# Compressed keys and values of a hybrid decoder step: two tokens stacked on 128 rows, and the first attention scores laid between the stages

## The reference, cut to what matters

```
def nsa_compress(rows, w1, w2, pe):              # rows: tokens x 64, once for keys, once for values
    n_cmp = (L - CMP_LEN) // CMP_STRIDE + 1      # CMP_LEN = 32, CMP_STRIDE = 16
    idx = arange(n_cmp)[:, None] * CMP_STRIDE + arange(CMP_LEN)[None, :]
    blocks = rows[:, idx] + pe                   # windows of 32 tokens
    h = gelu(einsum('bnld,ldh->bnh', blocks, w1))    # w1: 32 x 64 x 128
    return einsum('bnh,hd->bnd', h, w2)              # w2: 128 x 64
```

## Time and profile before

| | us |
|---|---|
| median of 3 runs (lowest, highest) | 1422.31 (1421.23, 1422.4) |
| the profiled execution: its time | 1421.6 |
| its span, first to last instruction | 1419.7 |
| PE busy | 1290.8 (91%) |
| DVE busy | 712.4 (50%) |
| ACT busy | 405.0 (29%) |
| POOL busy | 177.3 (12%) |

### The profile page before, as it was taken

One profiled execution on the slowest core, in us unless ns is written; L12 is line 12 of the kernel. 1 busy time (PEld: TensorE's weight loads), 2 busy tenths in 40 slices (PEclk: granted clock), 3 DMA queues, 4 the chain that ended last, 5 costly groups with the idle time before them and its releaser, 6 DMA issues.

```text
span 1419.7 us, 19519 instructions
## 1 busy us (share of the span) xinstructions
PE 1290.8 (91%) x6942; PEld 774.6 (55%) x6942; DVE 712.4 (50%) x1629; ACT 405.0 (29%) x858; POOL 177.3 (12%) x209
## 2 busy tenths in 40 slices
PE   3699999999999999979999999999828999999966
PEld 1568787787877545646666765545323333333322
DVE  5526575574854101247676674253752333333339
ACT  3132232332421200115665664132201111111016
POOL 0003121030221000200000000000001222211132
PEclk9699999999999999969999999999958999999988
DMA  9802011040111205204300004500167968495855
GB/s 315 256 18 60 16 40 37 18 75 0 34 59 46 97 0 90 94 8 95 111 18 9 1 1 134 168 34 27 65 232 260 317 241 292 156 333 161 280 178 222
DMA packets 123238, 163.19 MB, mean 115 GB/s; under 512 B 29763, under 2 KB 98547, under 8 KB 123160
## 3 DMA queue, kind: packets, MB, share of 16 engines
q1 hardware_dynamic: 108840, 112.75, 26.1%
q0 software_dynamic: 14320, 49.41, 10.1%
HBM read 225.01 MB, written 36.45 MB: 184 GB/s over the span
## 4 chain that ended last, share of the span: by engine, by line
PE 79%; DVE 13%; DMA 3%; ACT 2%; issue 2%; POOL 0%; SPq 0%; DVEq 0%; POOLq 0%; ACTq 0%
PE act L652 16%; PE vec L1159 11%; PE vec L919 9%; PE vec L681 7%; PE vec L853 5%; PE vec L702 4%; PE act L865 4%; PE act L877 2%; PE act L1172 2%; PE vec L1172 2%; PE act L884 2%; DMA arena<-x_rows,arena 2%; PE vec L817 1%; PE vec L662 1%; PE act L1139 1%
## 5 line engine op out<-in xcount | busy, mean ns | idle before, releaser
L652 PE MATMUL act<-arena 128*128 128x352 f32 x768 | 240.2, 469 | 0.4 <-issue 0.4
L652 PEld LDWEIGHTS act<-arena 128*128 128x128 f32 x768 | 146.0, 194 | 77.6 <-issue 4.6
L1159 PE MATMUL vec<-arena 128*64 128x512 f32 x768 | 172.4, 601 | 2.5 <-issue 2.5
L919 PE MATMUL vec<-arena 128*128 128x512 f32 (+1 forms) x288 | 126.3, 593 | 0.4 <-ACT arena L1357 0.4
L1795 DVE CUSTOM_DVE_ANT_0 arena<-vec,arena 128x128 f32<-128x128 f32 (+9 forms) x200 | 86.8, 459 | 59.8 <-PE vec L853 49.7
L1159 PEld LDWEIGHTS vec<-arena 128*64 128x64 f32 x768 | 54.2, 138 | 103.9 <-issue 103.5
L681 PE MATMUL vec<-arena 128*128 128x512 f32 (+1 forms) x256 | 99.9, 546 | 0.0
L2087 DVE TENSOR_SCALAR arena<-arena 128x256 f32<-128x256 f32 x24 | 7.1, 296 | 170.7 <-ACT arena L1468 170.7
L919 PEld LDWEIGHTS vec<-arena 128*128 128x128 f32 (+1 forms) x288 | 50.8, 180 | 67.6 <-issue 66.3
L1370 ACT COPY arena<-act 128x512 f32<-128x512 f32 (+11 forms) x176 | 63.6, 431 | 81.3 <-PE act L865 81.3
L1377 ACT ACTIVATE arena<-arena 128x640 f32<-128x640 f32 (+15 forms) x128 | 81.6, 644 | 16.5 <-DVE arena L1795 16.5
(11 more groups left out here) (378 smaller groups left out, 1873.0 us busy)
## 6 DMA issues: line engine op xcount, KB each, us to landing
arena<-in_exp_w SPq DMA_DIRECT2D x144, 1024.0 KB
y_rows<-arena POOLq DMA_DIRECT2D x48, 256.0 KB, 5.1
arena<-in_w_in SPq DMA_DIRECT2D x16, 512.0 KB, 7.0
arena<-in_x_prompt SPq DMA_DIRECT2D x8, 512.0 KB, 8.9
x_spill<-arena POOLq DMA_DIRECT2D x8, 512.0 KB, 5.7
arena<-x_spill SPq DMA_DIRECT2D x8, 512.0 KB, 5.5
arena<-in_cache_fox_kv SPq DMA_DIRECT2D x16, 256.0 KB, 3.4
x_rows<-arena POOLq DMA_DIRECT2D x8, 512.0 KB, 2.9
```

Source lines behind the costliest of these rows:

```text
L652: last = mm(bk[:, 0:n], W[k % 2][:, c, m * P:(m + 1) * P], xT[:, c, a:a + n], start=c == 0, stop=c == NC - 1)
L919: last = mm(bk[:r], src, Wo[:, c, half * 512:(half + 1) * 512], start=c == 0, stop=c == NC - 1)
L1159: last = mm(gu_bank[p][o], xgT[p][:, c, o], Wgu[:, slot, c, :], start=c == 0, stop=c == NC - 1)
```

## The change

Two neighbouring tokens are stacked: rows 0 to 63 hold even tokens, rows 64 to 127 odd ones, keys and values in two planes of a new buffer, `tokens2`. The first layer is then 16 matmuls of 128 rows for keys and 16 for values, in place of 64 of 64 rows. Keys' hidden values come first, then the decay rows of head 0, then the values' hidden values; the rest of the compression is laid between the first steps of attention. The cached rows are loaded before `w1c`, which is loaded in four parts; the position rows are turned after the first sparse tile, the cached ones within the loop of tiles. The GELU is done for keys and for values apart (183 columns each). `cumf` and `foxdiag` move behind `S` and `PT` in memory.

```diff
@@ the stream of SP @@
-        e.wait_ge(*E.at(("w_in used", 5)))
-        e.dma_start(w1c[0:64], I["nsa_cmp_w1"][0, 0].rearrange("l d x -> d l x")).then_inc(*E.moved("cmp_in"))
-        e.dma_start(w1c[64:128], I["nsa_cmp_w1"][0, 1].rearrange("l d x -> d l x")).then_inc(*E.moved("cmp_in"))
...
         for n in range(DB * NP):
             e.dma_start(KVT[:, n // NP, n % NP, :], nkp[page_of(n), :, 0:2].rearrange("a p k d -> p (a k d)")).then_inc(*E.moved("cmp_cache_in"))
-        e.wait_ge(*E.at("KC ready"))
+        e.wait_ge(*E.at(("w_in used", 5)))
+        for kv in range(2):
+            for odd in range(2):
+                src = I["nsa_cmp_w1"][0, kv].rearrange("(j two) d x -> two d j x", two=2)
+                e.dma_start(w1c[64 * odd:64 * odd + 64, kv], src[odd]).then_inc(*E.moved("cmp_in"))
+        e.wait_ge(*E.at("VC ready"))
@@ the stream of PE @@
         for t in range(NT):
             token_tile(t, W_nkvg, 400, 6)
+            if t == 0:
+                e.wait_ge(*E.at("cmp_in"))
+                e.wait_ge(*E.free("vec"))
+                bk = E.bank("vec")
+                e.transpose(bk[:, 0:32], pe_sb[0:32, :], ident[0:32, 0:32]).then_inc(*E.filled("vec"))
+                e.wait_ge(*E.at("cmp_cache_in"))
+            if t % 2 and t < 8:
+                turn_cached_keys(t - 1)
             if t >= 2:
                 turn_sparse_keys(t - 2)
-        e.wait_ge(*E.at("cmp_cache_in"))
-        for b in range(0, DB, 2):
...
         turn_sparse_keys(7)
...
-        for l in range(32):
-            for kv in range(2):
-                s = slice(64 * kv, 64 * kv + 64)
-                last = mm(hidden_banks[kv][:, 0:WINDOWS], w1c[s, l, :], skew(kcvc[s, :], l, [16, WINDOWS]), start=l == 0, stop=l == 31)
+        def hidden_values(kv):
+            e.wait_ge(*E.free("vec"))
+            bk = E.bank("vec")
+            for j in range(16):
+                last = mm(bk[:, 0:WINDOWS], w1c[:, kv, j, :], skew(tokens2[:, kv, :], j, [8, WINDOWS]), start=j == 0, stop=j == 15)
+            last.then_inc(*E.filled("vec"))
...
+        hidden_values(0)
+        e.wait_ge(*E.at("LF ready"))
+        decay_rows(0)
+        hidden_values(1)
         E.stage("attn")
-        e.wait_ge(*E.at("KC ready"))
...
-        decay_rows(0)
         for d in range(n + 3):
+            if d == 1:
+                compressed_keys()
+                e.wait_ge(*E.at("KC ready"))
+            if d == 4:
+                e.wait_ge(*E.at("VC ready"))
             if d < n:
                 scores(d)
+                if d == 1:
+                    compressed_values()
@@ the stream of ACT @@
-            e.copy(KVT[:, b:b + 2].rearrange("p b j n -> p (b j n)"), bk).then_inc(*E.drained("act", "KVT ready"))
+            for kv in range(2):
+                turned = bk[64 * kv:64 * kv + 64].rearrange("p (t two) -> p t two", two=2)
+                for odd in range(2):
+                    last = e.copy(tokens2[64 * odd:64 * odd + 64, kv, at:at + PAST], turned[:, :, odd])
@@ the stream of DVE @@
+        def pairs_of(bk, n, at):
+            for kv in range(2):
+                turned = bk[64 * kv:64 * kv + 64, 0:n].rearrange("p (t two) -> p t two", two=2)
+                for odd in range(2):
+                    last = cp(tokens2[64 * odd:64 * odd + 64, kv, at // 2:(at + n) // 2], turned[:, :, odd])
...
-            cp(kcvc[:, t * P:(t + 1) * P], bk[:, 0:P]).then_inc(*E.done())
+            pairs_of(bk, P, t * P).then_inc(*E.done())
...
+        gelu_inner(0)
         decay_rows(0)
+        gelu_outer(0)
+        gelu_inner(1)
         for it in range(n + 1):
+            if it == 1:
+                compressed_keys()
             if it < n:
                 scores(it)
+                if it == 1:
+                    gelu_outer(1)
+                    compressed_values()
```

More of the change, by code:

```diff
@@ L267, in program @@
     w2, w2d, pe_sb, pc = z.take(2 * P, 2), z.take(2 * P), z.take(P), z.take(2)
-    w1c = z.take(32 * P, 32)
+    w1c = z.take(32 * P, 2, 16)
     tail = 53200 - 2 * 4096 - NC * NTOK
@@ L777, in turn_sparse_keys, with turn_cached_keys @@
             bk = E.bank("vec")
-            for j, a in enumerate((0, 64, 192)):
-                last = e.transpose(bk[:, j * P:(j + 1) * P], nkvg[:, t, a:a + P], ident)
+            for n, a in enumerate((0, 64, 192)):
+                last = e.transpose(bk[:, n * P:(n + 1) * P], nkvg[:, t, a:a + P], ident)
             last.then_inc(*E.filled("vec"))
+        def turn_cached_keys(b):
+            e.wait_ge(*E.free("act"))
+            bk = E.bank("act")
+            for n in range(4):
+                last = e.transpose(bk[:, n * P:(n + 1) * P], KVT[:, b + n // NP, n % NP, :], ident)
+            last.then_inc(*E.filled("act"))
         e.wait_ge(*E.at(("w_in", 5)))
@@ L829, in _ @@
[L829 to L833, removed]
+        e.wait_ge(*E.at("pairs by vec"))
+        e.wait_ge(*E.at("pairs by act"))
+        def hidden_values(kv):
+            e.wait_ge(*E.free("vec"))
+            bk = E.bank("vec")
+            for j in range(16):
+                last = mm(bk[:, 0:WINDOWS], w1c[:, kv, j, :], skew(tokens2[:, kv, :], j, [8, WINDOWS]), start=j == 0, stop=j == 15)
+            last.then_inc(*E.filled("vec"))
@@ new lines, in compressed_keys, with compressed_values @@
+        def compressed_keys():
+            e.wait_ge(*E.at(("cmp hidden", 0)))
+            e.wait_ge(*E.free("vec"))
+            bk = E.bank("vec")
+            mm(bk[:, 0:HALF_GELU], w2d[:, 0:P], gx[:, 0:HALF_GELU], start=True, stop=True).then_inc(*E.filled("vec"))
+        def compressed_values():
+            e.wait_ge(*E.at(("cmp hidden", 1)))
+            e.wait_ge(*E.free("vec"))
+            bk = E.bank("vec")
+            v = gx[:, HALF_GELU:]
+            mm(bk[:NCMP, 0:64], v[:, 0:NCMP], w2[:, 1, 0:64], start=True, stop=True).then_inc(*E.filled("vec"))
+            e.wait_ge(*E.free("vec"))
+            bk = E.bank("vec")
+            for b in range(DB):
+                last = mm(bk[:NCMPS, b * 64:(b + 1) * 64], v[:, NCMP + 15 * b:NCMP + 15 * b + 15], w2[:, 1, 0:64], start=True, stop=True)
+            last.then_inc(*E.filled("vec"))
@@ L1334, in _ @@
             bk = E.job("act")
[L1335 removed]
+            at = (NTOK + b * PAST) // 2
+            for kv in range(2):
+                turned = bk[64 * kv:64 * kv + 64].rearrange("p (t two) -> p t two", two=2)
+                for odd in range(2):
+                    last = e.copy(tokens2[64 * odd:64 * odd + 64, kv, at:at + PAST], turned[:, :, odd])
+                    last.then_inc(*(E.drained("act", "pairs by act") if kv and odd else E.done()))
         e.wait_ge(*E.at("gate logits"))
@@ L1343, in _ @@
         E.stage("p3")
[L1344 to L1348, removed]
+        for kv in range(2):
+            u = gu[:, kv * HALF_GELU:(kv + 1) * HALF_GELU]
+            e.wait_ge(*E.at(("gelu inner", kv)))
+            act(u, u, ACT.Exp, scale=-1.5957691216057308).then_inc(*E.done(("gelu exp", kv)))
         E.stage("attn")
@@ L1675, in _ @@
         e.memset(tmp9, 0.0).then_inc(*E.done())
+        def pairs_of(bk, n, at):
+            for kv in range(2):
+                turned = bk[64 * kv:64 * kv + 64, 0:n].rearrange("p (t two) -> p t two", two=2)
+                for odd in range(2):
+                    last = cp(tokens2[64 * odd:64 * odd + 64, kv, at // 2:(at + n) // 2], turned[:, :, odd])
+                    if not (kv and odd):
+                        last.then_inc(*E.done())
+            return last
         def sparse_keys_turned(t):
@@ L1733, in gelu, with compressed_keys, compressed_values @@
             e.wait_ge(*E.own())
-            tt(x, x, u, ALU.mult).then_inc(*E.done(tag))
-        for kv in range(2):
+            tt(x, x, u, ALU.mult).then_inc(*E.done(("cmp hidden", kv)))
+        def compressed_keys():
             e.wait_ge(*E.full("vec"))
             bk = E.job("vec")
[L1739 to L1756, removed]
+            cp(KC[64:128, 0:NCMP], bk[64:128, 0:NCMP]).then_inc(*E.done())
+            cp(KCs[64:128, :], bk[64:128, NCMP:HALF_GELU]).then_inc(*E.drained("vec", "KC ready"))
+        def compressed_values():
+            e.wait_ge(*E.full("vec"))
+            bk = E.job("vec")
+            cp(VC[:NCMP, :], bk[:NCMP, 0:64]).then_inc(*E.drained("vec"))
+            e.wait_ge(*E.full("vec"))
+            bk = E.job("vec")
+            cp(VCs[:NCMPS], bk[:NCMPS].rearrange("p (b d) -> p b d", b=DB)).then_inc(*E.drained("vec", "VC ready"))
         E.stage("attn")
```

62 lines of the change are left out of this document (25 added, 37 removed).

## The result

The changed kernel took 1426.56 us (median of 9 runs, 1423.87 to 1432.01), the kernel before 1422.40 in the same series: ratio 1.0036, 95% interval 1.0023 to 1.0048. It is slower by 0.4%; 1415.6 and a gain were forecast. A later series gave 1.0043 (1.0030 to 1.0056) again. The profiled execution took 1432.01, the longest of its nine, with a span of 1429.9.

The account below looks back on a forecast made before the run. PE, busy 1290.8 of 1419.7 us, and the gaps in its path bound the kernel. +13.2 up to T0 and -19.9 from there to the first transpose gave -6.7: 1414.9, as median 1415.6; range 1409.5 to 1420.8.

Parts of the forecast that it names:

- The stall and the clock behind it: After the first sparse tile, PE waits 7.8 us for `w1c`; the low clock afterwards loses 2.5 us.
- Up to T0: From p2b's start to T0, PE's first first-layer matmul: stall, clock, moved work and tail together add 13.2 us.
- the 0.8 for a clock that falls ahead of T0: PE idles about 3 us ahead of the first-layer matmuls; the clock may fall, adding 0.8 us, half its 1.6 cost.
- Moved transposes and the tail: Cached and position-row transposes in the tile loop add 2.0 us; DVE's copies after the last tile add 0.1.
- The first layer: Compression's first layer: stacked 128-row matmuls cost 0.33 us each, so each group of 16 takes 5.3 us.
- A rule against the halving: First layer: 128-row and 64-row matmuls cost the same per column (1.70 and 1.71 ns), so half the number takes half the time.
- The rival in which the halving gives nothing: First layer: 64-row pairs already overlapped, so 10.6 us of saving are missing and the time is 1426; chance 0.01.
- From T0 to the first transpose otherwise: From the first first-layer matmul to attention's first transpose: 22.2 us in place of 42.15, saving 19.9.
- The mask on POOL: Before attention's first minimum: costs nothing if 16 output issues keep 9 us; rival with 14 us gives 1420.6, chance 0.12.
- Later stages are unchanged: Everything from attention's first transpose on runs as before, adding no time.
- The rival in which the clock recovers earlier there: In attention, up to 3.2 us more come back; with the stall at its lower bound, about 1411; chance 0.18.
- The slower rival I named: Behind the `w1c` stall the clock stays low for 24 us, costing 12 in place of 2.5: 1425; chance 0.06.

Follow-up runs that it names:

- e6: The changed kernel with stacked tokens laid out so each first-layer matmul reads neighbouring columns, copies scattering on writing; 1422.50 us, ratio 1.0002 to the kernel before.
- e5: The changed kernel with small weights and position rows counted apart, PE waiting for `w1c` only ahead of the first-layer matmuls; 1419.74 us, ratio 0.9981 to the kernel before.
- e7: The changed kernel with both repairs, the later `w1c` wait and the neighbouring-column token layout; 1413.89 us, ratio 0.9944 to the kernel before.
- e1: The kernel before with its 64 first-layer matmuls reordered, all 32 of the keys, then all 32 of the values; 1442.93 us.

## Why the prediction was wrong

Point by point, by its steps:

- **The stall and the clock behind it:** right. 7.69 us idle for 7.8, 3.2 us lost in the next tile for 2.5 (1.8 in e6), restart at 548.4 with the whole stage 3.1 us earlier than in the first profile. Up to T0 it is +13.3 for +13.2, and e5 gives the 10.8 back in its profile. That the total came out to 0.1 is luck: the 0.8 for a clock that falls ahead of T0 was not paid (it fell at 599.2, behind T0, where a step of 8 does not feel it), and the 0.7 more behind the stall stands in for it.
- **Moved transposes and the tail:** right. The last tile's end to T0 is 3.9 us (594.87 to 598.77) for the 3.7 of my working. DVE's copies set it; reading every second column of PSUM they follow each other at 0.23 us in place of 0.20, far from double.
- **The first layer:** this is the step that failed, the one I called "A rule against the halving". It read 1.71 ns a column for the 64-row matmuls and 1.70 for the tiles' and took them for the same price. They were equal by coincidence: 1.71 is twice the price, for the step of 16, and half of it, for running in pairs. Stacking gave up the pairs and kept the price of a wide step (0.70 us a matmul at step 8, 0.66 a pair at step 16). So the 32 cost 22.6 us, not 10.6: +12.0, which turns -6.7 into +5.3, against +4.2 measured. The row could not settle it, for it compared a contiguous 128-row operand with a strided 64-row one. The rival in which the halving gives nothing said 1426, and 1426.56 was measured; I had given it 0.01. Its mechanism was right. That its number fits so well is partly chance, for it has no term for attention's 6 us, of which the median shows little. The rule of the Trainium skill ("TensorEngine Tiling (Array Packing)", "Key Properties"), that different tiles run matmuls in parallel, is borne out: 21.18 us by turns, 40.92 in blocks.
- **From T0 to the first transpose otherwise:** right. 33.8 less the 12.0 are 21.8, for 22.2. The mask on POOL was no wait that mattered. In the changed kernel the 12 us of longer matmuls would have hidden one, so the test is e7: there the mask ended 15.4 us behind T0 and DVE wanted it at 17.2, and the 16 output issues kept their 9 us.
- **"Later stages are unchanged":** wrong by about 6 us in the profiles, by the clock in attention's start and at two changes of head. How much of it the executions without a profile had is not known. The rival in which the clock recovers earlier there went the other way.

The slower rival I named, a clock low for 24 us behind the stall, did not come: it was full again 6 us after PE went on. The range's lower edge, 1409.5, does not follow from the terms named for it (-3.5 from 1415.6 is 1412.1); its upper edge, 1420.8, had no term for the first layer.

## What to carry to other kernels

A group of matmuls that is as fast as it should be may be so for two reasons that cancel: before you restructure it, ask of the row what it reads by what step and which rows of the array its neighbours use, and compare only like with like. Here the cure was not the stacking but the layout: the same 64 matmuls took 10.8 us in place of 21.2 once each read neighbouring columns. And a wait on a counter takes everything that is counted on it: small loads that are wanted early belong on a counter of their own.

## What the runs showed of the hardware that was not expected

- A moving fp32 operand of 193 columns costs 0.34 us a matmul at steps 1 and 2, 0.51 at 3, and 0.68 to 0.70 at 4, 5, 6 and 8, at 2.4 GHz. At a step of 8 a low clock costs almost nothing (11.45 against 11.16 us for 16), at step 1 it nearly doubles the price (0.65).
- The clock can fall while PE works without a gap: in e1 it fell at 593.3, 4.2 us into the 64 matmuls at step 16, and stayed at 1.2 GHz through the rest of them; in the kernel before, with the same matmuls in pairs, it stayed at 2.4. Why is open.
- Matmuls on rows 0 to 63 and 64 to 127, by turns and into different banks, run side by side at step 1 (0.17 us each) and at step 16 (0.33 each); in blocks of one half they don't (0.64).
- DVE's scaling waits for POOL. In the changed kernel two of them, of 512 columns, took 0.88 us with POOL idle, and 2.21 us with POOL's mask beside them, of which the first took 2.06:

```profile
710.19 0.88 DVE L1844 TENSOR_SCALAR arena<-arena 128x512 f32<-128x512 f32 x2
717.64 2.00 POOL L2238 TENSOR_TENSOR arena<-arena 128x1024 f32<-128x1024 f32 x1 [58.28 <-DVE arena L1838]
717.86 2.21 DVE L1844 TENSOR_SCALAR arena<-arena 128x512 f32<-128x512 f32 x2
720.13 1.33 PE L871 MATMUL act<-arena 128*128 128x128 f32 x5 [2.10 <-DVE arena L1844]
```

This wait ends PE's gap of 1.8 to 2.1 us at each change of head, behind which the clock may fall. The Trainium skill ("SBUF — State Buffer", "Who interferes with whom") has only this pair of engines contend; the rows agree.
